# Routing reordered, expert loads moved, and the first expert tile as native fp32 products

## The reference

```python
x = x + jnp.concatenate([conv_out, gla_out], axis=-1) @ w_out[l]
hf = rmsnorm(x, ffn_norm_g[l])
x = x + hier_moe(hf, ...)     # top-1 of 4 groups, then top-2 of its 8 experts, 32 experts in all
return rmsnorm(x, final_norm_g)
# one expert: (silu(xblk @ w_gate[e]) * (xblk @ w_up[e])) @ w_down[e]
# w_gate, w_up: 1024 x 512; w_down: 512 x 1024; every token goes to 2 experts
```

## Time and profile before

| | us |
|---|---|
| median of 3 runs | 1046.96 (1046.01 to 1047.67) |
| profiled execution | 1045.44 |
| its span in the trace | 1043.7 |
| mean granted clock of TensorE in it | 0.964 |

### The profile page before, as it was taken

How to read it: one execution, slowest core, us unless ns; L and a number is a source line. 1 busy time by engine, 2 the same in 40 slices (tenths; PEclk the granted TensorE clock), 3 DMA queues, 4 the chain that set the end, 5 groups by cost and what they waited for, 6 DMA issues and landing times.

```text
span 1043.7 us, 12148 instructions
## 1 busy us (share of the span) xinstructions
PE 952.9 (91%) x4539; PEld 679.0 (65%) x4539; DVE 663.0 (64%) x752; ACT 461.0 (44%) x554; POOL 329.4 (32%) x245
## 2 busy tenths in 40 slices
PE   7999999999999998499998999899999898998961
PEld 5758888887878886375655554556664677874541
DVE  5468999988786767784553154325342598965554
ACT  6576456344562223353343134214242467744451
POOL 0275998933120000122222212122221223431133
PEclk9989999999999999599999999999999999999986
DMA  9620202020073324789999999899999999989964
GB/s 320 178 82 1 81 1 81 0 82 1 1 263 121 111 92 161 268 325 371 394 407 352 387 413 405 317 365 377 356 354 411 399 409 404 380 320 374 367 244 182
DMA packets 65294, 264.97 MB, mean 254 GB/s; under 512 B 10853, under 2 KB 29477, under 8 KB 40656
## 3 DMA queue, kind: packets, MB, share of 16 engines
q1 hardware_dynamic: 51792, 237.07, 57.7%
q0 software_dynamic: 10032, 18.60, 7.1%
q10 hardware_dynamic: 3408, 8.48, 2.1%
HBM read 249.44 MB, written 28.84 MB: 267 GB/s over the span
## 4 chain that ended last, share of the span: by engine, by line
PE 35%; DMA 15%; DVE 5%; ACT 2%; issue 2%; POOL 0%; SPq 0%; POOLq 0%; ACTq 0%; DVEq 0%
PE ps L2289 8%; PE ps L2262 7%; PE ps L2264 7%; PE ps L2263 7%; DMA raw<-in_expert_w_up_dram 4%; DMA raw_b<-in_expert_w_up_dram 4%; PE ps L2302 3%; DMA raw<-in_expert_w_gate_dram 3%; PE ps L2255 2%; DMA summed_rows<-ym,idx_g 1%; ACT hi_a L1232 1%; DVE lo_a L1794 1%; ACT junk L1314 1%; DMA xg<-hf_rows,idx_g 1%; DMA gate_col<-gate_rows,idx_s 1%
## 5 line engine op out<-in xcount | busy, mean ns | idle before, releaser
L2262 PE MATMUL ps<-hi_a,xm_hi 128*128 128x512 f32 x304 | 124.6, 410 | 19.7 <-DVE lo_b L1794 8.6
L2264 PE MATMUL ps<-hi_a,xm_lo 128*128 128x512 f32 x304 | 123.3, 406 | 0.0
L853 POOL DMA_INDIRECT summed_rows<-ym,idx_g x25 | 52.1, 2082 | 208.5 <-DVE ym L1843 208.5
L2289 PE MATMUL ps<-raw_b,xm 128*64 128x512 f32 x256 | 113.6, 600 | 3.3 <-DMA raw<-in_expert_w_up_dram 3.3
L2289 PE MATMUL ps<-raw,xm 128*64 128x512 f32 x256 | 113.5, 600 | 1.2 <-DMA raw_b<-in_expert_w_up_dram 1.2
L1794 DVE TENSOR_TENSOR lo_a<-raw,hi_a 128x2048 fp32r<-128x2048 f32 x32 | 72.8, 2293 | 39.7 <-ACT hi_a L1232 39.7
L1405 DVE SCALAR_TENSOR_TENSOR ps<-uT,pcol,ps 128x1024 f32<-128x1024 f32 (+1 forms) x87 | 96.5, 1109 | 2.4
L764 POOL TENSOR_TENSOR acc<-x,acc 128x1024 f32<-128x1024 f32 x30 | 85.3, 2843 | 30.8 <-ACT x L1024 26.6
L1794 DVE TENSOR_TENSOR lo_b<-raw_b,hi_a 128x2048 fp32r<-128x2048 f32 x28 | 63.6, 2289 | 47.3 <-ACT hi_a L1232 47.3
L838 POOL DMA_INDIRECT xg<-hf_rows,idx_g x27 | 33.3, 1234 | 173.3 <-PE ps L2255 150.9
L2262 PEld LDWEIGHTS ps<-hi_a,xm_hi 128*128 128x128 f32 x304 | 58.8, 193 | 38.1 <-DVE lo_b L1794 10.3
(11 more groups left out here) (366 smaller groups left out, 2321.8 us busy)
## 6 DMA issues: line engine op xcount, KB each, us to landing
raw_b<-in_expert_w_gate_dram SPq DMA_DIRECT2D x32, 1024.0 KB
raw_b<-in_expert_w_up_dram SPq DMA_DIRECT2D x32, 1024.0 KB, 12.3
raw<-in_expert_w_up_dram SPq DMA_DIRECT2D x32, 1024.0 KB
raw<-in_expert_w_gate_dram SPq DMA_DIRECT2D x32, 1024.0 KB, 10.3
raw_b<-in_expert_w_down_dram SPq DMA_DIRECT2D x32, 1024.0 KB
raw<-in_expert_w_down_dram SPq DMA_DIRECT2D x32, 1024.0 KB
raw<-in_w_in_dram SPq DMA_DIRECT2D x8, 1024.0 KB, 6.8
xa<-in_x_dram SPq DMA_DIRECT2D x8, 512.0 KB, 8.8
```

The costliest lines, as they stand in the source:

```text
L853: return pool.indirect_dma_start(out=sum_dram, out_offset=bass.IndirectOffsetOnAxis(ap=at.bitcast(U32), axis=0), in_=src, in_offset=None, ...
L2262: pe.matmul(dst, x_hi, w_h, start=first, stop=False)
L2264: return pe.matmul(dst, x_lo, w_h, start=False, stop=stop)
L2289: last = pe.matmul(ps[r * BL:(r + 1) * BL, i // 2, :], xm[:, kk, r * BL:(r + 1) * BL], slot(n, i)[:, w], start=(kk == 0), stop=(kk == KC - 1))
```

## The change

The order of the tiles is changed in two places: tile 0 is of a new kind N, and the last P goes from place 24 to 23. `up_pair` and `down_pair` become `up_native` and `down_native`, which take one expert on all 128 columns too; `split_first` goes. In the routing, `residual(t)` is put before `choose(t - 1)`, and the ranking becomes a function that DVE calls after its half of the copy of tile 0. (0,4), (0,5) and (1,4), (1,5) are issued at other places, and `sum_out` counts the stores of tiles 0 to 3 and 4 to 7 instead of the even and the odd ones.

```diff
-    KINDS = "SSPSPDEPSPDEPDEPSPSSSSSSPSS"
+    KINDS = "NSPSPDEPSPDEPDEPSPSSSSSPSSS"
@@ planned_loads
-                    split = 0.0 if KINDS[t] == "P" else T_SPLIT
+                    split = T_SPLIT if is_split(t) else 0.0
-                    end += (T_PAIR if KINDS[t] == "P" else T_ONE) + ...
+                    end += (T_ONE if is_split(t, "SDE") else T_PAIR) + ...
@@ SP
-            for t in range(2, NT):
+            for t in range(2, NT - 1):
                 load_x(t)
+            sp.wait_ge(ss_rdy, NT + 4)
+            sp.wait_ge(xt_ps, 8)
+            sp.wait_ge(hf_rdy, 4)
+            sp.wait_ge(sum_out[0], 16 * (NT // 2))
+            load_expert(0, 4, 0)
+            load_expert(0, 5, 0)
+            load_x(NT - 1)
             sp.wait_ge(w_used, 1)
             load_expert(1, 2, 1)
             load_expert(1, 3, 1)
             sp.wait_ge(x2_rdy, NT)
             load_expert(0, 3, 0)
             load_expert(1, 0, 1)
             load_expert(1, 1, 1)
-            for b in range(2):
-                sp.wait_ge(hf_out[b], 16 * (NT // 2))
-                sp.wait_ge(sum_out[b], 16 * (NT // 2))
-            load_expert(0, 4, 0)
-            load_expert(0, 5, 0)
-            sp.wait_ge(g_in, 16)
             load_expert(1, 4, 1)
             load_expert(1, 5, 1)
@@ ACT
-                act.dma_start(sum_v[t], x2[:, t, :]).then_inc(sum_out[t % 2], 16)
+                act.dma_start(sum_v[t], x2[:, t, :]).then_inc(sum_out[t // (NT // 2)], 16)
-                    split_first(0) ... split_first(3)
             def x_hi(t):
                 if first(t):
                     act.wait_ge(x0_ps, 1)
-                    (both halves to xm_hi, each when its transposes are done)
-                    return
-                act.wait_ge(xgt_ps, t + 1)
-                act.wait_ge(split_used, after_piece(t - 1, 3))
-                if KINDS[t] == "P":
+                else:
+                    act.wait_ge(xgt_ps, t + 1)
+                    act.wait_ge(split_used, after_piece(t - 1, 3))
+                if isinstance(t, int) and KINDS[t] in "PN":
                     act.activation(xm[:, 0:4, :] ..., ps[:, 2, :], ACT.Copy).then_inc(xh_rdy, 1)
@@ DVE
+            residual(0)
             for t in range(1, NT):
-                residual(t - 1)
                 normed(t - 1)
                 if t + 1 < NT:
                     conv_columns_lo(t + 1)
                 if t >= 2:
                     place(t - 2)
                 if t + 1 < NT:
                     gla_columns_lo(t + 1)
-                if t == NT - 1:
-                    split_first(1)
+                    residual(t)
                 choose(t - 1)
-                if t == NT - 2:
-                    split_first(0)
             residual(NT - 1)
@@
+            def ranked():
                 (the ranking of the 30 experts, L1718 to L1728, as it was)
             def begin():
                 x_lo(0)
-                split_first(2)
-                split_first(3)
+                ranked()
                 columns()
@@ PE
+            def up_native(places, i):
+                m = P // len(places)
+                for n in places:
+                    pe.wait_ge(*slot_in(n, i))
                 for k in range(4):
                     kk, w = 4 * (i % 2) + k, slice(k * F, (k + 1) * F)
+                    for r, n in enumerate(places):
+                        last = pe.matmul(ps[r * m:(r + 1) * m, i // 2, :], xm[:, kk, r * m:(r + 1) * m], slot(n, i)[:, w],
                                          start=(kk == 0), stop=(kk == KC - 1))
                 last.then_inc(split_used, 1)
@@ gate_up
-                if first(t):
-                    pe.wait_ge(x0l_rdy, 1)
+                native = KINDS[t] in "PN"
+                if native:
+                    pe.wait_ge(xh_rdy, t + 1)
+                if not first(t):
                     pe.wait_ge(xl_rdy, t + 1)
                 for i in range(4):
                     if first(t) and i == 1:
                         pe.wait_ge(xl_rdy, 1)
```

More of the change, by code:

```diff
@@ L565, in n_split_tiles @@
         def n_split_tiles(t):
-            return sum(k != "P" for k in KINDS[:t + 1])
+            return sum(is_split(v, "SDE") for v in range(t + 1))
         def added_at(t):
@@ L1261, in hidden_hi @@
                 act.wait_ge(ht_ps, t + 1)
-                dst = hmT if isinstance(t, int) and KINDS[t] == "P" else hm_hi
+                dst = hmT if isinstance(t, int) and KINDS[t] in "PN" else hm_hi
                 act.activation(dst[:].rearrange("p j i -> p (j i)"), ps[:, 4, :], ACT.Copy).then_inc(hh_rdy, 1)
@@ L1869, in step @@
                     rows_out(t - 1)
-                if KINDS[t] != "P":
+                if is_split(t, "SDE"):
                     hidden_lo(t)
@@ L2287, in up_pair, with down_native @@
                     kk, w = 4 * (i % 2) + k, slice(k * F, (k + 1) * F)
-                    for r, n in enumerate(pair):
-                        last = pe.matmul(ps[r * BL:(r + 1) * BL, i // 2, :], xm[:, kk, r * BL:(r + 1) * BL], slot(n, i)[:, w],
+                    for r, n in enumerate(places):
+                        last = pe.matmul(ps[r * m:(r + 1) * m, i // 2, :], xm[:, kk, r * m:(r + 1) * m], slot(n, i)[:, w],
                                          start=(kk == 0), stop=(kk == KC - 1))
                 last.then_inc(split_used, 1)
-            def down_pair(pair, i):
-                for n in pair:
+            def down_native(places, i):
+                m = P // len(places)
+                for n in places:
                     pe.wait_ge(*slot_in(n, i))
@@ L2300, in down_pair @@
                         w = slice(k * D + h * 512, k * D + (h + 1) * 512)
-                        for r, n in enumerate(pair):
-                            last = pe.matmul(ps[r * BL:(r + 1) * BL, 5 + h, :], hmT[:, kk, r * BL:(r + 1) * BL], slot(n, i)[:, w],
+                        for r, n in enumerate(places):
+                            last = pe.matmul(ps[r * m:(r + 1) * m, 5 + h, :], hmT[:, kk, r * m:(r + 1) * m], slot(n, i)[:, w],
                                              start=(kk == 0), stop=(kk == FC - 1))
@@ L2306, in gate_up @@
             def gate_up(t):
-                pair = KINDS[t] == "P"
-                if first(t):
-                    pe.wait_ge(x0l_rdy, 1)
-                else:
-                    if pair:
-                        pe.wait_ge(xh_rdy, t + 1)
+                native = KINDS[t] in "PN"
+                if native:
+                    pe.wait_ge(xh_rdy, t + 1)
+                if not first(t):
                     pe.wait_ge(xl_rdy, t + 1)
@@ L2316, in gate_up @@
                         pe.wait_ge(xl_rdy, 1)
-                    if pair:
-                        up_pair(tile_pos[t], i)
+                    if native:
+                        up_native(tile_pos[t], i)
                     else:
@@ L2337, in down @@
                 for i in (4, 5):
-                    if pair:
-                        down_pair(tile_pos[t], i)
+                    if native:
+                        down_native(tile_pos[t], i)
                     else:
```

56 lines of the change are left out of this document (16 added, 40 removed).

## The result

Median 1030.49 us (1029.86 to 1036.42, 4 runs) against 1047.32 (1046.01 to 1048.95, 4 runs) of the kernel before beside it: the medians differ by -16.8 us, the ratio of the means is 0.9851 [0.9812, 0.9890]. The forecast was -7.1, to 1039.8, with a range of 1034.5 to 1045. Three later timings of the same changed kernel, each against the kernel before on its chip, gave ratios of 0.9845, 0.9882 and 0.9917 (medians -16.6, -13.8 and -9.1 us). The direction was right, the size was not, and -16.8 is the largest of the four.

What follows compares the result with a forecast made beforehand. PE, busy 952.9 of 1043.7 us, bounds the kernel, with full DMA queues in the expert stage; time is won where PE stands still. Front -2.7 and tail -4.4 give -7.1 us, to 1039.8, range 1034.5 to 1045.

Steps and rivals of the forecast that it cites:

- the first gather's: Before the expert stage: tile 7's store, held by loads, lands near 431.0; gather issued at 431.9 (was 433.32), landing -5.65 us.
- Rival 1: Store not held by loads, lands by 425; gather lands at 434, PE's tail waits gone; 1034 to 1037 us; chance 0.14.
- Routing: Last residual 4.4 us earlier, at 412.75; expert 0's row numbers at 428.3 instead of 432.72; bounds 2.2 and 5.5.
- The gather alone: First gather without loads (0,4) and (0,5) beside it takes 3.6 us instead of 7.83; bounds 3.3 and 7.8.
- The native tile: Tile 0: native records at 0.427 us each cost PE +2.5 us in the up part and +1.2 in the down part.
- Rival 3: Tile 0: a native record on 128 columns costs 0.618 us; front +6.5, total +2.1 us, 1049; chance 0.07.
- Front in sum: From tile 2 on: -5.65 gather landing, -0.74 dropped `lo`, +2.5 and +1.2 native products, -2.7 us; bounds -6.5 and +5.
- The tail: Kernel's end: pair one place earlier removes the second scatter, -5.4, with +1.0 of PE waits: -4.4 us; bounds -7 and 0.
- Rival 2: Kernel's end: PE waits in tiles 24 and 25 take back all 5.4 us; only the front counts, 1044.2; chance 0.17.

Runs made afterwards that it cites:

- loads_at_store: Changed kernel with SP waiting for the last normed rows, so all five expert loads start together with tile 7's store; 1036.01 us, 0.9921 of the kernel before.
- store_alone: Changed kernel with the five expert loads issued only when all stores of hf_rows have landed; 1037.83 us, 0.9930 of the kernel before.
- before: The kernel before, unchanged, in its first trace; profiled execution 1045.44 us, median of the timing beside the changed kernel 1047.32 us.
- after: The changed kernel in its first trace; profiled execution 1029.86 us, median 1030.49 us, 0.9851 of the kernel before.
- no_native: Changed kernel with tile 0 split again and its four weight splits back on ACT and DVE; 1035.62 us, 0.9911 of the kernel before.
- pair_back: Changed kernel with the last pair back at place 24 instead of 23; 1040.88 us, 0.9950 of the kernel before.
- before_again: The kernel before, unchanged, timed and profiled a second time; 1049.56 us against 1046.05, ratio 1.0039 for the same code.
- pair_back_2: Changed kernel with the last pair back at place 24, timed again on one chip with after_third; 1040.04 us, 0.9930 of the kernel before.
- pair_only_2: The kernel before with only the last pair moved from place 24 to 23, timed again with five rounds; 1040.99 us, 0.9945 of the kernel before.
- after_again: The changed kernel, unchanged, timed and profiled a second time; 1030.47 us, 0.9845 of the kernel before.
- after_third: The changed kernel, unchanged, timed on one chip with pair_only_2 and pair_back_2; 1033.31 us, 0.9882 of the kernel before.

## Why the prediction was wrong
**The failed step is the first gather's.** The prediction said: "if the store waits for them as tile 7's did it lands near 431.0, no earlier than before. So the store, not the routing, becomes last, and of 4.4 us I keep 1.4". Measured: the store landed at 424.5, half a microsecond ahead of the row numbers; in the twelve traces of the changed kernel and its variants that have loads beside it, it took 6.9 to 8.8 us, alone 2.7. I had read a wait for all loads out of the earlier trace rows, 7.6 us beside 2.6. The packets tell what it was. The store's first packet of data moves 3.4 to 4.2 us behind its issue where three or five loads are ahead of it, 2.1 us behind in `loads_at_store` and 0.8 in `store_alone`; what sets that first wait stays open. Then both queues move data at once. In the kernel before three loads were nearly through by then, so the rest went almost alone and the whole looked like a wait; in the changed kernel the store shared the engines with the loads and still landed ahead of two of them. Its time hardly depends on how many MB there are. Rival 1 had this mechanism and got a chance of 0.14. A slip of the sum made the term worse: five loads from 414.1 at 12.6 to 13.3 us end at 426.7 to 427.4, not at 428.5.

Behind the row stood a rule: the Trainium skill, DMA: Bandwidth & Descriptors, section Queues, rings and completion order, has both the round of packets between the queues and the strict order of the completion. The traces agree with the first: from 420 to 424 us of the changed kernel q1 moved 1.15 MB and q10 0.56. The second doesn't make a store wait until all loads issued ahead of it are done (8.2 us, two of the five landing later); what it does within an engine no run here shows.

**Routing.** Predicted -4.4 us, bounds 2.2 and 5.5. From store 5 to store 7 it was -4.8, and the step from there to the gather -0.5. The term was right for this pair of traces, and its whole amount reached the gather. The other three traces with the old routing have 31.8 to 31.9 us where `before` has 30.4; against them the stretch is 6.2 us shorter, beyond the upper bound of 5.5. The last residual's 410.01 is 7.1 us earlier than before, of which 2.4 are A, so 412.4 by the old A: the forecast was 412.75.

**The gather alone.** Predicted 3.6 us, measured 5.2 (bounds 3.3 and 7.8). The sums' store and the last loads were still beside it. Landing was forecast at -5.65; it came -10.35, or -7.95 without A: 3.9 more by the store that was not last, 1.6 less by the gather.

**The native tile.** Predicted +2.5 and +1.2 us with 0.427 us a record. The records follow one another at 0.43 us: 6.87 us for 16, and 14.98 for 32 with the clock at 0.50 in their first 2.2 us. Between transposes this shows as +1.5 at tile 0 and +1.3 at its down part. Rival 3 (0.618 us) is refuted: the grouping of after has 634 ns in mean for a record of tile 0's up part, as the earlier trace rows has 618, but they overlap and follow at 0.43. What I missed is on DVE: the room that the removed splits give to the late ranking, 4.2 us at tile 1 (`no_native`).

**Front in sum.** Predicted -2.7 us at tile 2, measured -7.55, or -5.15 without A.

**The tail** was mis-sized. I took the second scatter with its step, -5.4, and +1.0 for new waits. From tile 26 on four traces with the pair at 24 have 66.5 to 71.0 us, twelve with it at 23 have 59.7 to 63.1: in mean 68.9 and 61.3, so -7.6. From tile 21 to 26 the same traces give 104.8 and 105.8, the +1.0 as predicted. The sum is -6.5 for -4.4. The term was sized on one of two kinds of execution. Where tile 24's scatter took 6.2 to 6.9 us (`before`, `pair_back`), the stretch from tile 26 on is 67.3 and 66.5 us, 5.6 above the 61.3, as the forecast's 5.4; where it took 9.7 to 9.8 (`before_again`, `pair_back_2`), it is 71.0 and 70.6, 9.5 above. There `ym_b` comes 9.5 and 9.7 us behind PE's last transpose of hidden rows, in `before` 6.7, so 4 us of slack were left there, not 1.3. Rival 2 is refuted: by the medians of `pair_only_2` and `pair_back_2` the pair is worth 6.1 and 6.7 us. The kernel before was profiled in an execution with a short tail (169.6; the other three with the pair at 24 have 172.7 to 176.8), from which I sized the term.

**What no step had.** A lies at 315.8 to 316.8 in eight of the seventeen traces and at 318.3 to 319.6 in nine, in code that none of them changed. The changed kernel has both groups, twice each, so the -2.4 us of the first pair of traces is not the change's; the last section shows where they arise. The middle, with the pair at 23 or not, runs from 375.4 to 381.1; where A is early it is 376.6 in mean, where late 379.4. Of its -5.7, 1 to 2 us can be the pair's (in mean over the traces with the pair at 23 the middle is 377.6, at 24 it is 379.4; 17 to 21 alone 86.2 and 87.2); the rest is of the size by which the changed kernel differs from itself (375.4 to 380.7). Against that the profiled execution of the kernel before had the shortest front and tail of its kind (174.5, where the same code took up to 178.7, and 169.6), so the first pair of traces shows too little there and too much elsewhere. In the middle the granted clock is a part of what varies: it was at its low level for 3.4 to 13.7 us of the stage, in mean 8.1 us in the traces with an early A and 11.4 in those with a late one. What the rest is stays open.

In means over the traces: four of the changed kernel against the four of the old front code give 169.1 for 176.8, -7.7; the tail against the four with the pair at 24 167.3 for 173.6, -6.3; together -14.0 where the forecast had -7.1. The four timings lie at -9.1 to -16.8, in mean -14.1. The range reached to 1034.5, the rival to 1034 to 1037; both were too narrow for an error of the same sign in front and tail. The terms were sized on an execution that was short in both of the stages in question. That the medians of the first timing differ by as much as 16.8 us has luck in it: that timing, like `after_again`, caught the changed kernel with an early A.

No run beat the changed kernel clear of noise: each part that was undone beside it on one chip made it slower or left it the same. For `no_native` and `pair_back` it was not on the chip; their ratios, 0.9911 and 0.9950, lie within and above the 0.9845 to 0.9917 of its own.

## What to carry to other kernels
A transfer that is slow beside others may share or may wait. Before building on one of them, look whether a transfer issued ahead of it lands behind it, and count each queue's packets in the same stretch: a sharer moves data while the others do. Two fixes of one wait are not to be added, and work taken off an engine is priced with all that newly stands behind it. A single trace gives terms, but stages that the change doesn't touch should be allowed their own spread, here 2.5 and 5 us.

## What was not expected of the hardware
**The start of the output projection falls in two groups 2.5 us apart, and TensorE's granted clock makes part of the step.** The groups part between the eighth and the ninth of POOL's 30 additions for the convolution, at 73 to 84 us. ACT and DVE there copy what eight small matmuls of PE give, in `after` and then in `after_third`:
```profile
68.92 3.67 PE L1982 MATMUL ps<-lowT,gkw 16*128 16x512 f32 x8 [0.86 <-DVE lowT L1427]
```
```profile
69.97 5.29 PE L1982 MATMUL ps<-lowT,gkw 16*128 16x512 f32 x8 [0.86 <-DVE lowT L1427]
```
In all eight traces with an early A the granted clock stays at 1.0 (2.4 GHz) and the eight take 3.67 us, 0.43 each; in all nine with a late one it falls to 0.5 (1.2 GHz) among them, from there each takes 0.85, and the eight take 5.2 to 6.0. PE had stood still for 0.86 us before them in all seventeen. ACT's copies wait for the eight, and the ninth addition, which stands behind ACT's work, comes 1.0 to 1.7 us later. What the rest of the 2.5 us is, and why the clock falls in one execution and not in the other, is open.

**A gather is as sensitive as a store.** 512 KB by the first gather took 4.7 to 5.5 us behind the early loads, 7.9 to 8.8 with two issued just ahead of it, 8.9 and 9.1 in the midst of five; tile 7's 512 KB store took 2.7 us alone and 6.9 to 8.8 beside loads. The order of the issues decides which of the two pays.
